# A two-layer hybrid trunk on one core: the expert rows of layer 1's two closing positions are added from on-chip memory by one-hot products

## The reference, cut to what matters

```python
idx = top-2 experts inside each token's best group
w = aff[idx] / sum(aff[idx])
gates = sum(one_hot(idx) * w)                      # (tokens, 16), two entries per token are not zero
out = zeros
for e in range(16):
    he = silu(t @ w_gate[e]) * (t @ w_up[e])       # 1024 -> 512
    out = out + gates[:, e:e + 1] * (he @ w_down[e])   # 512 -> 1024
h_lat = h_lat + g_f * out
```

## Time and profile before

| | us |
|---|---|
| median of 3 runs | 1327.61 |
| runs | 1323.94, 1327.61, 1327.64 |
| the profiled execution: its time | 1324.65 |
| the profiled execution: its span | 1322.8 |
| TensorE busy | 1154.3 (87%) |
| VectorE busy | 398.0 (30%) |
| ScalarE busy | 219.0 (17%) |
| GpSimd busy | 136.1 (10%) |
| mean granted TensorE clock | 0.944 of full |

### The profile page before, as it was taken

How to read it: one execution, slowest core, us unless ns; L and a number is a source line. 1 busy time by engine, 2 the same in 40 slices (tenths; PEclk the granted TensorE clock), 3 DMA queues, 4 the chain that set the end, 5 groups by cost and what they waited for, 6 DMA issues and landing times.

```text
span 1322.8 us, 17678 instructions
## 1 busy us (share of the span) xinstructions
PE 1154.3 (87%) x7340; PEld 648.3 (49%) x7340; DVE 398.0 (30%) x748; ACT 219.0 (17%) x416; POOL 136.1 (10%) x118
## 2 busy tenths in 40 slices
PE   3899998999999399999999099998999489999872
PEld 1444444776644245644554055645764264655440
DVE  0131124894422722221211522115732521111002
ACT  2120221112311211101010212221121211101000
POOL 0002201640000100000000301113300000000001
PEclk8899999989999799999999599999998789999996
DMA  9321115643452389999995521327427489999994
GB/s 378 142 88 63 65 63 216 243 155 121 151 231 80 124 336 355 415 426 423 425 426 181 198 105 63 121 79 295 175 79 303 161 340 370 423 425 426 426 426 138
DMA packets 34800, 319.40 MB, mean 241 GB/s; under 512 B 6560, under 2 KB 7712, under 8 KB 17056
## 3 DMA queue, kind: packets, MB, share of 16 engines
q1 hardware_dynamic: 22432, 292.03, 55.0%
q10 hardware_dynamic: 7392, 13.64, 2.9%
q0 software_dynamic: 4896, 12.59, 2.7%
HBM read 308.79 MB, written 14.69 MB: 245 GB/s over the span
## 4 chain that ended last, share of the span: by engine, by line
PE 78%; DMA 11%; DVE 7%; ACT 2%; issue 2%; SPq 0%; POOL 0%; ACTq 0%; DVEq 0%; POOLq 0%
PE ps L829 14%; PE ps L1171 13%; PE ps L1200 7%; PE ps L1073 6%; PE ps L816 6%; PE ps L1174 4%; DMA ring<-in_w_mod 3%; DMA tokA<-in_w_down 3%; PE ps L762 3%; DMA tokA<-in_w_gate 2%; PE ps L1177 2%; PE ps L986 2%; PE ps L1209 2%; PE ps L1148 2%; PE ps L1002 2%
## 5 line engine op out<-in xcount | busy, mean ns | idle before, releaser
L829 PE MATMUL ps<-ring,featT 128*128 128x512 f32 (+1 forms) x480 | 186.9, 550 | 0.0
L829 PEld LDWEIGHTS ps<-ring,featT 128*128 128x128 f32 x480 | 90.7, 190 | 92.3 <-issue 89.9
L1171 PE MATMUL ps<-arena 128*64 128x256 f32 x896 | 105.3, 389 | 5.8 <-ACT arena L1465 2.4
L2002 DVE TENSOR_TENSOR arena<-arena,ps 128x256 f32<-128x256 f32 (+2 forms) x32 | 15.6, 488 | 255.0 <-PE ps L1171 131.5
L1171 PEld LDWEIGHTS ps<-arena 128*64 128x64 f32 x896 | 65.0, 140 | 43.7 <-issue 16.4
L1073 PE MATMUL ps<-ring,featT 128*128 128x512 f32 x192 | 82.7, 592 | 0.0
L816 PE MATMUL ps<-featT,ring 128*128 128x512 f32 (+1 forms) x192 | 80.5, 577 | 2.3 <-ACT featT L1290 2.3
L2010 DVE COPY arena<-ps 128x512 f32<-128x512 f32 (+2 forms) x32 | 26.4, 824 | 156.3 <-PE ps L1200 79.6
L2206 POOL DMA_INDIRECT arena<-ffn_rows,slot_i x22 | 24.1, 1094 | 410.9 <-DVE slot_i L1994 410.9
L1472 ACT ACTIVATE arena<-ps 128x256 f32<-128x256 f32 (+2 forms) x32 | 14.0, 437 | 313.4 <-PE ps L1171 160.6
L1174 PE MATMUL ps<-arena 128*128 128x512 f32 x128 | 58.0, 608 | 2.3 <-ACT arena L1465 2.3
(11 more groups left out here) (298 smaller groups left out, 1596.5 us busy)
## 6 DMA issues: line engine op xcount, KB each, us to landing
ring<-in_w_mod SPq DMA_DIRECT2D x21, 2048.0 KB, 8.2
arena<-in_w_up SPq DMA_DIRECT2D x20, 2048.0 KB, 17.1
arena<-in_w_gate SPq DMA_DIRECT2D x16, 2048.0 KB, 18.7
ring<-in_w_down SPq DMA_DIRECT2D x12, 2048.0 KB, 13.5
arena<-in_w_down SPq DMA_DIRECT2D x12, 2048.0 KB, 17.6
ring<-in_w_in SPq DMA_DIRECT2D x10, 2048.0 KB, 7.9
ring<-in_w_gate SPq DMA_DIRECT2D x8, 2048.0 KB, 17.5
ring<-in_w_out SPq DMA_DIRECT2D x4, 2048.0 KB, 8.4
```

The source lines that it names most:

```text
L829: o = mm(bank[:, lo:hi], featT[:, k, P * i:P * i + P], W[:, k, lo:hi], start=k == 0, stop=k == KD - 1)
L1171: o = mm(ps[64 * half:64 * half + 64, m, 0:256], X_[:, k, at:at + SMALL_CAP], W[:, k, 256 * half:256 * half + 256], start=k == 0, stop=k = ...
```

## The change

Layer 1 has two "joined" positions, 14 and 15. Their rows don't go to `expert_rows` any more. VectorE multiplies them by `grow` on their way out of PSUM into `Yb`. A one-hot matrix that says which slot a token has, times the token's gate for that expert, is made by VectorE (`weigh_slots`), turned by TensorE (`turn_slots`, four transposes) and copied by ScalarE (`slot_rows`). TensorE multiplies it by the rows in `Yb` (`join`, four products of 64 x 128 by 64 x 512 for each position), both positions summed in PSUM, and VectorE adds the sum to `h` (`add_joined`).

The other rows are gathered from the table as before, but GpSimd now waits only for the stores of positions 12 and 13. For a token whose expert is joined the index points to the row of zeros. The gathered rows go to buffers that are free by then (`back_joined`), and VectorE's three operations on each tile (`add_gathered`) stand ahead of the result copies of positions 14 and 15 in its order. In layer 1 the turned rows `hT` have two buffers, and position 15 is turned ahead of `down(14)`; `down(15)` writes another PSUM bank. Some semaphores of the start of the program are merged, with the same meaning.

```diff
+        back_joined = [gathered[0], h[:, 0, :], diag[:, 1, :], h[:, 1, :]]
+        hT_joined = [hT, moved[:, 2 * NE:4 * NE, :].rearrange("p a b -> p (a b)").rearrange("p (a b) -> p a b", a=4)]
...
-        PLANS = [Plan(*TIERS[l], ORDERS[l]) for l in range(DEPTH)]
+        PLANS = [Plan(*TIERS[l], ORDERS[l], (NE - 2, NE - 1) if l == DEPTH - 1 else ()) for l in range(DEPTH)]
...
                 def down(r, q):
                     pe.wait_ge(S("hT_act"), r.all * NE + (q + 1))
+                    last = q == NE - 1 and q in plan.joined
                     if q > 0:
-                        pe.wait_ge(S("y_dve"), r.all * NE + q)
+                        pe.wait_ge(S("y_dve"), r.all * NE + (q - 1 if last else q))
                     W = weights(r, q, 2, 4)
+                    to = 4 if last else 3
...
+                def turn_slots(r):
+                    pe.wait_ge(S("row_steps"), r.all * 22 + (n_round * 4 + 26))
+                    pe.wait_ge(S("who_dve"), r.units + len(units))
+                    for j in range(2):
+                        for i in range(T):
+                            c = P * (T * j + i)
+                            o = tr(ps[:, 7, c:c + P], slot_gate[:, j, i, :], ident)
+                    o.then_inc(S("join_pe"), 1)
+
+                def join(r, q):
+                    j = plan.joined.index(q)
+                    pe.wait_ge(S("slots_act"), n_round + 1)
+                    pe.wait_ge(S("y_dve"), r.all * NE + (q + 1))
+                    for i in range(T):
+                        for half in range(2):
+                            s = slice(64 * half, 64 * half + 64)
+                            o = mm(joined_sum(i)[:, 512 * half:512 * half + 512], slot_rows[s, j, i, :],
+                                   Yb[s, q % 2, 0:512], start=j == 0, stop=j == 1)
+                        if j == 1:
+                            o.then_inc(S("join_pe"), 1)
...
+                        if plan.joined and q == NE - 1:
+                            turn_h(r, q)
                         if q > 0:
                             down(r, q - 1)
+                        if plan.joined and q == NE - 4:
+                            turn_slots(r)
-                    turn_h(r, NE - 1)
+                    if not plan.joined:
+                        turn_h(r, NE - 1)
                     down(r, NE - 1)
+                    for q in plan.joined:
+                        join(r, q)
...
                 def turned_h(r, q):
-                    if q > 0:
-                        act.wait_ge(S("dn_pe"), r.all * NE + q)
+                    held = 2 if plan.joined else 1
+                    if q >= held:
+                        act.wait_ge(S("dn_pe"), r.all * NE + (q + 1 - held))
...
                 def result(r, q):
+                    if q in plan.joined:
+                        for half in range(2):
+                            s = slice(64 * half, 64 * half + 64)
+                            o = V.tensor_tensor(Yb[s, q % 2, 0:512], ps[s, 3 + q % 2, :], grow[s, 1, 512 * half:512 * half + 512], ALU.mult)
+                        o.then_inc(S("y_dve"), 1)
+                        return
...
+                def weigh_slots(r):
+                    v = plan.joined[0]
+                    mv = moved[:, 0:2 * T, :].rearrange("p (t j) e -> p t j e", t=T)
+                    V.tensor_tensor(mv, gates[:, t0:NT, :].unsqueeze(2).to_broadcast([P, T, 2, NE]),
+                                    perm[:, v:v + 2, :].unsqueeze(1).to_broadcast([P, T, 2, NE]), ALU.mult
+                                    ).then_inc(S("row_steps"), 1)
...
+                    V.tensor_reduce(gate_last, mv, AX.X, ALU.add).then_inc(S("row_steps"), 1)
...
+                    for j in range(2):
+                        for i in range(T):
+                            o = V.tensor_scalar(slot_gate[:, j, i, :].rearrange("p (a s) -> p a s", a=2), repeat(const[:, C_IOTA:C_IOTA + SMALL_CAP], 2),
+                                                placeR[:, t0 + i, v + j:v + j + 1], gate_last[:, i, j:j + 1], ALU.is_equal, ALU.mult)
...
+                def add_gathered(i):
+                    dve.wait_ge(S(f"back{q % 4}"), backs(l, q, first, n_round))
+                    dve.wait_ge(S("half_act"), ended(l, first, n_round, i + 1))
+                    V.scalar_tensor_tensor(sum_, back_joined[q], gate2[:, 0, t:t + 1], sum_, ALU.mult, ALU.add
+                                           ).then_inc(S("both_dve"), 1)
...
+                    V.tensor_tensor(sum_, sum_, grow[:, t // 2, :], ALU.mult).then_inc(S("gated_dve"), 1)
...
+                    V.tensor_tensor(h[:, t, :], h[:, t, :], sum_, ALU.add).then_inc(S("gated_dve"), 1)
+
+                def add_joined(i):
+                    dve.wait_ge(S("join_pe"), n_round * 3 + (i + 2))
+                    V.tensor_tensor(h[:, t, :], h[:, t, :], joined_sum(i), ALU.add).then_inc(S("h_end"), 1)
...
                     pool.wait_ge(S("row_dve"), r.all + 1)
-                    pool.wait_ge(S("up_pe"), r.all * NE + NE)
+                    if plan.joined:
+                        pool.wait_ge(S("xT_pe"), r.units + (len(units) - 1))
+                    else:
+                        pool.wait_ge(S("up_pe"), r.all * NE + NE)
                     for c in range(2):
-                        pool.wait_ge(S(f"stored{c}"), r.stores + plan.stores(NE - 1))
+                        pool.wait_ge(S(f"stored{c}"), r.stores + plan.stores(NE - 2 + c))
```

More of the change, by code:

```diff
@@ L539, in no_row @@
             def no_row(self):
-                return sum(self.cap(v) for v in range(NE))
+                return sum(self.cap(v) for v in range(NE - len(self.joined)))
             def stores(self, q):
-                return 16 * sum(2 if self.small(p) else 6 if self.middle(p) else 1 for p in range(q % 2, q + 1, 2))
+                return 16 * sum(2 if self.small(p) else 6 if self.middle(p) else 1 for p in range(q % 2, q + 1, 2)
+                                if p not in self.joined)
             def runs(self):
@@ L550, in runs @@
                 return [(a, b, self.ranks[a]) for a, b in zip(starts, starts[1:] + [NE])]
-        PLANS = [Plan(*TIERS[l], ORDERS[l]) for l in range(DEPTH)]
+        PLANS = [Plan(*TIERS[l], ORDERS[l], (NE - 2, NE - 1) if l == DEPTH - 1 else ()) for l in range(DEPTH)]
+        for q in PLANS[DEPTH - 1].joined:
+            assert PLANS[DEPTH - 1].small(q) and PLANS[DEPTH - 1].ranks[q] == q
         N_TURN = 24
@@ L1506, in experts @@
                             turned_x(r, u + 1)
-                        if q > 0:
+                        if q > 0 and q - 1 not in plan.joined:
                             store(r, q - 1)
+                        if plan.joined and q == NE - 4:
+                            act.wait_ge(S("join_pe"), n_round * 3 + 1)
+                            A(slot_rows.rearrange("p j t s -> p (j t s)"), ps[:, 7, :], ACT.Identity).then_inc(S("slots_act"), 1)
                     turned_h(r, NE - 1)
-                    store(r, NE - 1)
+                    if not plan.joined:
+                        store(r, NE - 1)
                     for i in range(T):
@@ L2020, in step @@
                         ins.then_inc(S("row_steps"), 1)
-                        dve.wait_ge(S("row_steps"), r.all * STEPS + counted[0])
+                        dve.wait_ge(S("row_steps"), r.all * STEPS + (n_round * 4 + counted[0] if extra else counted[0]))
                     ch = chosen[:, 0:4 * T, :].rearrange("p (t g) e -> p t (g e)", t=T)
@@ L2081, in experts @@
                             who(r, u + 2)
+                        if plan.joined and q == NE - 1:
+                            add_gathered(0)
                         if q > 0:
                             result(r, q - 1)
+                        if plan.joined and q == 3:
+                            weigh_slots(r)
+                    if plan.joined:
+                        add_gathered(1)
                     result(r, NE - 1)
-                    add_rows(n_round)
+                    if plan.joined:
+                        for i in range(T):
+                            add_joined(i)
+                    else:
+                        add_rows(n_round)
                     dve.wait_ge(S("h_end"), NT + ended(l, first, n_round, T))
```

55 lines of the change are left out of this document (38 added, 17 removed).

## The result

The changed kernel takes 1318.76 us (median of 6 runs, 1309.05 to 1322.31), the kernel before on the same chips 1326.81 us. The ratio is 0.9937, with a 95% interval of 0.9912 to 0.9963: about 8 us faster. The profiled execution has a time of 1317.74 us and a span of 1315.9 us, 6.9 us less than before.

What follows compares the result with a forecast made beforehand. Bound by weight streaming to about 1292 us, then by a serial chain through down(15), store, gathers and VectorE. VectorE starts 14.6 earlier, its tail is 15.3 instead of 7.5: net 6.8, 1324.65 - 6.8 = 1317.9, given as 1319, range 1313 to 1323.5.

Steps and rivals of the forecast that it cites:

- The limit at which the kernel turns slower: Gather 1 landing from 1303.7 on, 12.7 us behind its issue, makes VectorE's 7.8 us longer tail a loss; slower case 0.06.
- the row with idle DMA engines: Lower end for gather 1's landing: 5.04 us in the kernel before, giving 1296.03; the forecast took 0.9 us over it.
- the 2 us of equal shares: If gathers and weights shared the DMA engines equally, the last weight would be late by up to 2 us.
- The upper bound: Upper end for gather 1's landing: 11.7 us, a mid-stream gather taken as equal in size, giving 1302.7; that rival's chance 0.14.
- the sixth that the prediction worked out: Gathers' share beside the weights under packet-by-packet turns: 2.7 of 16.3 parts, from 2.7 KB against 13.6 KB packets.
- The upper bound of 3.5 us more: If the joins' 64-row halves didn't overlap, a join takes 7 us at half clock and the end comes 3.5 us later.
- The half clock in join 15: TensorE, idle before the join, was taken at the 1.2 GHz level: 3.5 us for a join's four products, against 1.75.
- What costs nothing: weigh_slots (about 1.5 us), row-table step (0.2), turn_slots (0.5), removed stores, merged semaphores and second hT buffer add no time.
- the two rows: Profile rows behind the join's forecast: 0.44 us for a full-array 512-column pass, 0.44 us for eight 64-row passes of 128 columns.
- the 1322.8 us given for joins that don't overlap: The time that the forecast's own case was said to reach if the joins' halves didn't overlap; its own range was 1316 to 1321.5.
- the two places of three runs: The kernel before ran at 1323.94 and 1327.6; the changed median might fall in either, 1317.9 to 1320.8, so 1319 was given.

Runs made afterwards that it cites:

- e1: Changed kernel with GpSimd's gathers waiting for down(15) instead of only for the store of position 13; 1327.81 us, ratio 1.0005 to the kernel before.
- e2: Changed kernel with VectorE's order changed to result 14, gathered tile 0, result 15, gathered tile 1, joined additions; 1316.27 us, ratio 0.9908.
- e3: Changed kernel with seven unused products on TensorE, four between down(15) and join 14, three between the joins; 1318.51 us, ratio 0.9951.
- e7: Changed kernel with position 15 turned behind down(14) again, as in the kernel before; 1319.82 us, ratio 0.9941.
- e4: Kernel before with position 15's turn and copy ahead of down(14), a second hT buffer and another PSUM bank for down(15); 1323.9 us, ratio 0.9977.
- e5: e2 with layer 1 rows multiplied by grow as they leave PSUM and each gathered row added in one operation; 1311.94 us, ratio 0.9892.
- e6: e5 with the last addition and its output split into two halves of 512 columns; 1311.53 us, ratio 0.989.

## Why the prediction was right, step by step

The forecast was 1319 us (range 1313 to 1323.5), and 1318.76 us was measured. By the profiled executions, the saving was forecast as 6.8 us and came out as 6.9. The mechanism held, and the close numbers are in part luck (below).

| step | forecast | measured |
|---|---|---|
| store of position 13 lands | 1288.95 | 1289.31 |
| gather 0, gather 1 issued | 1289.73, 1290.99 | 1290.07, 1291.33 |
| gather 1 to landing | 5.94 | 5.73 |
| VectorE's first 128x1024 operation | 1297.1 | 1297.28 |
| each result as two 64x512 products | 1.4 | 1.38, 1.39 |
| down(15) starts | 1293.98 to 1296 | 1294.70 |
| join of eight passes at half clock | 3.5 | 3.78 busy, 3.8 in the chain |
| first 128x1024 operation to the end of the last addition | 15.3 | 15.56 |
| last addition to the end of the span | 3.5 | 3.06 |

*The gathers set the gain, VectorE's longer tail takes half of it back.* VectorE starts 14.46 us sooner (1311.74 - 1297.28) and ends its work 15.56 instead of 7.53 us later; the output is 0.47 us shorter. Together 6.9. e1 shows the same from the other side: without the early start nothing is won. The limit at which the kernel turns slower, a gather of 12.7 us, was never near, since the gather took 5.73 us.

*The landing.* Gather 1 landed at 1297.06 (1291.33 + 5.73), where I had 1296.9, near the row with idle DMA engines. In e1, where it ran with idle engines, it took 5.31 us, so the weights cost it 0.4. The last weight was held up by 0.2 us at most (e1), not by the 2 us of equal shares. The DMA queues of the changed kernel show a reason that I hadn't weighed, in three stretches (q1 has the weights, q0 the gathers): from 1290 to 1291 us, from 1291 to 1292 us, and from 1292 to 1292.8 us.

```profile
q1 hardware_dynamic: 22, 0.36, 84.0%
...
q1 hardware_dynamic: 22, 0.33, 76.6%
q0 software_dynamic: 3, 0.01, 7.6%
...
q1 hardware_dynamic: 17, 0.18, 53.0%
q0 software_dynamic: 19, 0.08, 38.8%
```

Gather 0 is issued at 1290.07, and nearly nothing of it moves before 1292; by then all but about 0.25 MB of the weights are through. The two hardly meet. Where they do, they send about as many packets each, 17 and 19, as the Trainium skill's rule of turns by packet has it ("DMA: Bandwidth & Descriptors", section "Queues, rings and completion order"). But the gathers have 0.08 of 0.26 MB there, not the sixth that the prediction worked out: the 2.7 KB of the earlier trace rows are a mean with two smaller gathers, and the four here move 2.10 MB in 576 packets, 3.6 KB each. That the short overlap keeps the weight on time is a reading of these rows, not a test.

The upper bound was misread too. The gather of 11.7 us in the stream isn't of the same size: from 1153 to 1165 us its queue moved 0.21 MB, and each of the four gathers here moves 0.52. So 11.7 us bounded nothing for 0.52 MB, and 11.7 against 5.04 can't be used for the rule. The forecast didn't hang on it, since its value was taken near the lower row.

*The clock and the tiles.* The join's halves did overlap: 1.99 us for eight passes at full clock (e2, e3), 0.25 each, where the full array takes 0.44. The upper bound of 3.5 us more fell away. The Trainium skill ("TensorEngine Tiling (Array Packing)", section "Key Properties") has a drain of the array at a change of tiling mode; what this case leaves for it and everything else is 0.25 us for a join (1.99 measured against 1.75 from the passes). The half clock in join 15 came as forecast and cost 1.45 us (e3).

*What costs nothing.* The place of the turn is slack (e7), though the turn with its buffers was worth 2.7 us in the kernel before (e4). `weigh_slots`, `turn_slots` and the merged semaphores weren't tried alone. `down(13)` starts 0.35 us later than before, within what kernels with the same code up to there show among themselves (1271.90 in e1, 1277.07 in e2), so nothing is put down to them.

*Where I was off.* The output behind the last addition was taken as unchanged, and it was 0.47 us shorter. It isn't chance: the stretch is 3.53 or 3.54 us in the two kernels with the old end (before, e4), 3.06 or 3.07 in the three with the changed kernel's (the changed kernel, e1, e7), and 3.27 to 3.29 where the two additions follow each other (e2, e3, e5). What made it so was not tried; e6 only shows that the size of the last transfer has little part in it. The join at half clock was 0.3 us longer than the two rows gave. And the 1322.8 us given for joins that don't overlap doesn't come out of the sum, which is 1317.9 + 3.5 = 1321.4.

*What was luck.* Misses cancel in the 0.1 us between 6.8 and 6.9: VectorE starts 0.14 us less early than forecast, its tail is 0.26 us longer, and the output is 0.47 us shorter. The 6.9 also holds the 0.35 us by which `down(13)` starts later, in executions that differ there by 5.9 us; from `down(13)` on, the saving is 7.25. And 1319 was picked between the two places of three runs, 1.1 us above the sum of 1317.9; no sum gives it.

The experiments point on: the order of e2 and the operations of e5 give 1311.94 us, with 7.5 us less from `down(13)` to the end than the changed kernel.

## What to carry to other kernels

When an operation at the end is moved forward, write down the order of the engine that takes its result. Here three operations, 3.8 us in all, stood ahead of result 14 and waited for a gather, while that result had already been ready for 3.8 us when they began (1297.28 - 1293.45); swapping them gained 4.0 us more by the profile. An edit has the worth of the path that it lies on: an early turn with its buffers was worth 2.7 us in one kernel, and its place in the order nothing in the next. And a product that waits for a slow chain pays twice, once for the wait and once for the clock that TensorE has lost meanwhile.

## What the runs showed of the hardware that was not expected

The executions differ long before the place of the change. A piece of the first large projection (48 passes, 20.7 us) starts at 69.23 us in the kernel before and at 72.47 us in the changed kernel. In e1, whose code is that of the changed kernel up to the end of layer 1, it starts at 69.55 us. Stretches of the kernel before, columns as above:

```profile
36.00:40.00 4.00, 2.58 (x20) 1.86 (x16) 0.54 (x3) 0.77 (x2) 0.00 (x0) 0.85 0.82 259
45.00:49.00 4.00, 3.46 (x8) 1.63 (x9) 0.43 (x1) 0.00 (x0) 0.00 (x0) 1.00 0.00 0
```

The same stretches of the changed kernel:

```profile
36.00:40.00 4.00, 3.30 (x19) 3.28 (x16) 0.00 (x0) 0.60 (x1) 0.00 (x0) 0.50 0.94 328
45.00:49.00 4.00, 2.86 (x7) 1.44 (x6) 1.00 (x2) 0.86 (x2) 0.00 (x0) 0.50 0.00 0
```

TensorE is at the 1.2 GHz level for longer here, with nearly the same work. Sixteen passes of one kind take 1.96 us from 37.33 in the kernel before and 3.59 us from 36.73 in the changed kernel. That is a part of the 3.2 us by which the two differ at 70 us. Which level these short bursts get at the start changes from one execution to the next: in the same two stretches the granted clock is 0.68 and 0.66 in e1 and 0.50 and 0.76 in e3, whose code is the same up to there as the changed kernel's 0.50 and 0.50. The 3.2 us don't last: at `down(13)` the changed kernel is only 0.35 us behind. `down(13)` started between 1271.90 and 1277.81 us in the ten profiled executions. So a change of 1.5 us at the end (e3) is seen in a profile and not in the times, and single runs of the changed kernel lie between 1309.05 and 1322.31 us. That the clock makes up all of this spread was not shown.

A gather of 512 KB spends part of its time before its first byte: the one issued at 1305.23 us in the kernel before, with idle DMA engines, took 4.2 us to land and moved no packet for the first 1.3 of them. The next three gathers took 5.0 to 5.3 us there and 5.3 to 5.9 us in e1, also behind the stream. Issued beside the last weights, gathers took 5.3 to 5.9 us in the seven kernels with early gathers, but for one of 7.3 us in e7, for which VectorE did not wait.
